# First two passes of an expert loop taken out ahead of the loop, with shared-expert work behind the first pass's gate and up products

## What is computed

```python
def swiglu(t, wg, wu, wd):
    return (jax.nn.silu(t @ wg) * (t @ wu)) @ wd
...
    def expert_block(args):
        tok, wb, e = args
        xb = t_pad[tok]
        yb = swiglu(xb, w_e_gate[e], w_e_up[e], w_e_down[e])
        return yb * wb[:, None]
...
    routed = jax.ops.segment_sum(yb.reshape(P, d), slot_tok, num_segments=T + 1)[:T]
    shared = swiglu(t, w_sh_gate, w_sh_up, w_sh_down)
    return (routed + shared).astype(h.dtype).reshape(b, n, d)
```

## Time and profile before

| what | value |
|---|---|
| median of 3 runs (lowest, highest) | 1037.86 us (1037.82 to 1041.65) |
| the profiled execution | 1042.4 us, its span 1040.6 us |
| busy in the span: PE, DVE, ACT, POOL | 944.7, 513.2, 330.9, 400.1 us |
| chain that ended last | PE 46%, DMA 43%, DVE 4%, SP's queue 4% |
| HBM read, written | 282.15 MB, 39.32 MB |

### The profile page before, as it was taken

How to read it: one execution, slowest core, us unless ns; L and a number is a source line. 1 busy time by engine, 2 the same in 40 slices (tenths; PEclk the granted TensorE clock), 3 DMA queues, 4 the chain that set the end, 5 groups by cost and what they waited for, 6 DMA issues and landing times.

```text
span 1040.6 us, 13867 instructions
## 1 busy us (share of the span) xinstructions
PE 944.7 (91%) x3980; PEld 388.6 (37%) x3981; DVE 513.2 (49%) x682; ACT 330.9 (32%) x595; POOL 400.1 (38%) x300
## 2 busy tenths in 40 slices
PE   3999999899999989979999898996999999999760
PEld 0554444466555553323333232332333333333220
DVE  2336876777156954434545344442445455454234
ACT  4212222377345422222232232322222323322232
POOL 0312431000000045553556644554455565555531
PEclk9999999999999999989999999998999999999895
DMA  9955452900314967999989999999999999999837
GB/s 368 350 181 202 167 198 71 363 1 2 122 81 156 356 230 284 394 388 377 382 294 339 397 381 370 373 357 367 387 377 362 352 354 372 370 355 366 308 71 243
DMA packets 63180, 298.29 MB, mean 287 GB/s; under 512 B 15189, under 2 KB 15905, under 8 KB 35121
## 3 DMA queue, kind: packets, MB, share of 16 engines
q1 hardware_dynamic: 42130, 258.01, 63.2%
q0 software_dynamic: 19024, 35.68, 14.2%
q10 hardware_dynamic: 2000, 4.28, 1.1%
HBM read 282.15 MB, written 39.32 MB: 309 GB/s over the span
## 4 chain that ended last, share of the span: by engine, by line
PE 46%; DMA 43%; DVE 4%; SPq 4%; issue 3%; ACT 1%; POOL 0%; ACTq 0%; POOLq 0%; DVEq 0%
DMA wring<-in_w_e_down 33%; PE psum L944 13%; PE psum L1186 10%; DMA wring<-in_w_e_up 5%; PE psum L1198 5%; PE psum L1034 3%; PE psum L981 3%; PE psum L1014 3%; PE psum L1005 2%; DMA ring<-in_w_ada 2%; SPq L451 2%; PE psum L1148 2%; DMA expert_sums<-xres,sidx 2%; SPq L427 1%; PE psum L899 1%
## 5 line engine op out<-in xcount | busy, mean ns | idle before, releaser
L1186 PE MATMUL psum<-wring,xres 128*64 x832 | 379.9, 611 | 35.5 <-DVE cur_g L1613 34.2
L1186 PE MATMUL psum<-cur_g,xres 128*64 128x512 f32 x832 | 379.9, 611 | 0.0
L554 POOL DMA_INDIRECT xg<-h_rows,gidx x216 | 249.6, 1156 | 219.4 <-ACT gidx L801 141.0
L1186 PEld LDWEIGHTS psum<-wring,xres 128*64 128x64 f32 x832 | 112.5, 140 | 258.4 <-issue 253.0
L1198 PE MATMUL psum<-wring,rows 128*64 x424 | 190.6, 592 | 1.9 <-ACT rows L797 1.9
L1198 PE MATMUL psum<-rows 128*64 128x512 f32 x424 | 190.7, 592 | 0.0
L1617 DVE STREAM_TRANSPOSE xres<-xg 128x1024 f32<-128x1024 f32 x53 | 108.5, 2047 | 160.9 <-DMA xg<-h_rows,gidx 158.7
L1613 DVE COPY cur_g<-wring 128x1536 f32 x106 | 125.7, 1228 | 46.3 <-SPq L440 46.3
L561 POOL DMA_INDIRECT expert_sums<-xres,sidx x54 | 95.4, 1767 | 96.9 <-DMA expert_sums<-xres,sidx 85.7
L862 ACT COPY xres<-psum 128x1024 f32<-128x1024 f32 x53 | 53.6, 1012 | 190.4 <-PE psum L1198 103.1
L1186 PEld LDWEIGHTS psum<-cur_g,xres 128*64 128x64 f32 x832 | 112.5, 140 | 0.0
(11 more groups left out here) (241 smaller groups left out, 870.1 us busy)
## 6 DMA issues: line engine op xcount, KB each, us to landing
wring<-in_w_e_gate SPq DMA_DIRECT2D x64, 1024.0 KB, 8.4
wring<-in_w_e_up SPq DMA_DIRECT2D x64, 1024.0 KB, 16.1
wring<-in_w_e_down SPq DMA_DIRECT2D x64, 1024.0 KB, 18.2
ring<-in_w_ada SPq DMA_DIRECT2D x20, 1024.0 KB, 5.1
ring<-in_w_in SPq DMA_DIRECT2D x4, 2048.0 KB, 29.1
heads<-in_w_ada SPq DMA_DIRECT2D x4, 1024.0 KB, 23.3
ring<-in_w_out SPq DMA_DIRECT2D x1, 4096.0 KB, 15.2
xg<-h_rows,gidx POOLq DMA_INDIRECT x216
```

Source lines behind the costliest of these rows:

```text
L554: pool.indirect_dma_start(xg[q][:, 256 * s:256 * s + 256], None, hrows, bass.IndirectOffsetOnAxis(gidx[:, q, s:s + 1].bitcast(U32), 0), bo ...
L1186: last = pe.matmul(pp[2][SUB * g:SUB * g + SUB, 512 * q:512 * q + 2 * F] .rearrange("p (u f) -> p u f", u=2), xT[:, q, k, SUB * g:SUB * g ...
```

## The change

PE: passes 0 and 1 are written out ahead of the loop, which now begins at pair 2. Pass 0 is gate and up alone; the absent pair's turn and down product are gone. `shared_hidden(3)` and `shared_down(3)` stand behind gate and up of pair 0 instead of ahead of it. ACT follows the same order: row numbers of gather 2 and the SiLU of pair 0 first, then `shared_keep(3)` and `shared_rows(3)`, then the wait for the stores, then the copies of pair 0's down weights. SP: load 6 also waits until gather 0 has landed (`s_gt[0]` at 64). DVE: the product of pair p's hidden values also waits for the turn of those before (`s_ht`). The last shared turn and down product count 2 instead of 1, so that all later counts stay as they were. POOL is unchanged, its wait for all four shared stores included.

```diff
@@ -491,6 +491,7 @@
                     down_arrived(n - 3)
                 if n == NB:
                     sp.wait_ge(s_gu, NT)
+                    sp.wait_ge(s_gt[0], 64)
                 else:
                     if n == NB + 1:
                         sp.wait_ge(s_tab, 1)
@@ -845,31 +846,44 @@
             shared_keep(2)
             shared_silu(3)
             shared_rows(1)
-            shared_keep(3)
             shared_rows(2)
-            shared_rows(3)
             act.wait_ge(s_idx, 1)
             act.wait_ge(s_tab, 1)
-            act.sem_inc(s_cdn, FJ)
             nb = act.value_load(ntab[0:1, 0:1], min_val=E, max_val=MAXB - 1)
             pairs = act.snap((nb + 1) // 2)
-            for n in range(1, NT):
-                act.wait_ge(s_sh_st[n], 16)
 
             def keep_y(n, q, scattered):
                 act.wait_ge(s_dn, n)
                 act.wait_ge(s_scat, scattered)
                 act.copy(ysb[:, q], pp[q]).then_inc(s_yev, 1)
 
-            with act.Fori(0, pairs, 2) as i:
+            def open_pass(p, q):
+                gather_index(p + 2, q)
+                w = down_weights(p)
+                act.wait_ge(s_gu, p + (NT + 1))
+                act.activation(sg, pp[2][:, 512 * q:512 * q + F], ACT.Silu).then_inc(s_sil, 1)
+                return w
+
+            def close_pass(p, q, w):
+                keep_y(p + (NT + 1), 1 - q, p * 16 + 16)
+                scatter_index(p - 1, 1 - q)
+                copy_down(*w)
+
+            w = open_pass(0, 0)
+            shared_keep(3)
+            shared_rows(3)
+            act.sem_inc(s_cdn, FJ)
+            for n in range(1, NT):
+                act.wait_ge(s_sh_st[n], 16)
+            act.sem_inc(s_yev, 1)
+            scatter_index(-1, 1)
+            copy_down(*w)
+            w = open_pass(1, 1)
+            close_pass(1, 1, w)
+            with act.Fori(2, pairs, 2) as i:
                 for q in range(2):
-                    gather_index(i + (q + 2), q)
-                    e, w0 = down_weights(i + q)
-                    act.wait_ge(s_gu, i + (q + NT + 1))
-                    act.activation(sg, pp[2][:, 512 * q:512 * q + F], ACT.Silu).then_inc(s_sil, 1)
-                    keep_y(i + (q + NT + 1), 1 - q, i * 16 + (16 * q + 16))
-                    scatter_index(i + (q - 1), 1 - q)
-                    copy_down(e, w0)
+                    w = open_pass(i + q, q)
+                    close_pass(i + q, q, w)
             turns = act.snap((pairs + 1) // 2)
             n_down = act.snap(turns * 2 + (NT + 1))
             n_scattered = act.snap(turns * 32 + 16)
@@ -1155,7 +1169,7 @@
                     pe.wait_ge(s_hte, n)
                 for j in range(FJ):
                     last = pe.transpose(pp[1][:, 512 + j * P:512 + (j + 1) * P], hmid_sh[:, j:F:FJ], ident)
-                last.then_inc(s_ht, 1)
+                last.then_inc(s_ht, 2 if n == NT - 1 else 1)
 
             def shared_down(n):
                 pe.wait_ge(s_hte, n + 1)
@@ -1170,7 +1184,7 @@
                     for j in range(FJ):
                         last = pe.matmul(o[:, 512 * m:512 * m + 512], hT_sh[:, n % 2, j, :],
                                          w[:, j, 512 * m:512 * m + 512], start=(j == 0), stop=(j == FJ - 1))
-                last.then_inc(s_dn, 1)
+                last.then_inc(s_dn, 2 if n == NT - 1 else 1)
 
             def weights_of(p):
                 e = pe.value_load(tab[0:1, bass.ds(p * 2 + 2, 1)], min_val=0, max_val=E - 1)
@@ -1232,24 +1246,37 @@
             shared_gate_up(3, range(5, KD))
             shared_down(1)
             shared_down(2)
-            shared_hidden(3)
-            shared_down(3)
             pe.wait_ge(s_tab, 1)
             nb = pe.value_load(ntab[0:1, 0:1], min_val=E, max_val=MAXB - 1)
             pairs = pe.snap((nb + 1) // 2)
+
+            def open_pass(p, q, w):
+                pe.wait_ge(s_xte, p + 1)
+                pe.wait_ge(s_w, w[0] + 2)
+                gate_up(p, q, w[1])
+
+            def full_pass(p, q, before, w):
+                pe.wait_ge(s_hm, p + NT)
+                turn_hidden(1 - q)
+                open_pass(p, q, w)
+                pe.wait_ge(s_hte, p + NT)
+                pe.wait_ge(s_yev, p + (NT - 1))
+                down(p * 2 + 1, 1 - q, *before)
+
+            w0 = weights_of(0)
+            pe.wait_ge(s_hm, NT)
+            open_pass(0, 0, w0)
+            shared_hidden(3)
+            shared_down(3)
+            w1 = weights_of(1)
             pe.wait_ge(s_yev, NT - 1)
-            with pe.Fori(0, pairs, 2) as i:
-                for q in range(2):
-                    before = (e, w0) if q else weights_of(i - 1)
-                    e, w0 = weights_of(i + q)
-                    pe.wait_ge(s_hm, i + (q + NT))
-                    turn_hidden(1 - q)
-                    pe.wait_ge(s_xte, i + (q + 1))
-                    pe.wait_ge(s_w, e + 2)
-                    gate_up(i + q, q, w0)
-                    pe.wait_ge(s_hte, i + (q + NT))
-                    pe.wait_ge(s_yev, i + (q + NT - 1))
-                    down(i * 2 + (2 * q + 1), 1 - q, *before)
+            full_pass(1, 1, w0, w1)
+            with pe.Fori(2, pairs, 2) as i:
+                before = weights_of(i - 1)
+                w = weights_of(i)
+                full_pass(i, 0, before, w)
+                w1 = weights_of(i + 1)
+                full_pass(i + 1, 1, w, w1)
             turns = pe.snap((pairs + 1) // 2)
             n_down = pe.snap(turns * 2 + NT)
             pe.wait_ge(s_hm, n_down)
@@ -1628,6 +1655,7 @@
                     e, w0 = gate_up_weights(i + (q + 1))
                     turn_block(1 - q, i * 32 + 64 * (q + 1))
                     dve.wait_ge(s_sil, i + (q + NT + 1))
+                    dve.wait_ge(s_ht, i + (q + NT))
                     dve.scalar_tensor_tensor(hmid, sg, slot_w[:, bass.ds(i + q, 1)],
                                              pp[2][:, 512 * q + F:512 * q + 2 * F], ALU.mult, ALU.mult)\
                        .then_inc(s_hm, 1)
```

## The result

| | before | changed |
|---|---|---|
| median of 16 runs each (lowest, highest) | 1039.12 us (1034.73 to 1043.42) | 1049.06 us (1044.11 to 1052.85) |
| the profiled execution, its span | 1042.4, 1040.6 us | 1047.97, 1045.9 us |

The ratio is 1.0097, 95% interval 1.0081 to 1.0112: 1% **slower**, 9.9 us. The forecast was 1036.5 in a range to 1041. The stage of the passes also begins 1.65 us earlier in the changed trace (first piece of gather 0 at 373.12, before 374.77); where it matters I count from that start, "from the stage's start".

What follows compares the result with a forecast made beforehand. Weight loads were taken to pace the passes, with PE full beside them. Of 4.1 us gained at the head, the late store and its waiters left 1.4 at pass 7: 1036.5 us, range 1031 to 1041.

Steps and rivals of the forecast that it cites:

- Gather 0 without g6: Head of the passes: with load 6 held back, the first gather lands at 382.7 us instead of 386.73.
- the 4.1: Head of the passes: gate and up of pair 0 start 4.1 us earlier, at 385.2.
- The upper bound of 5.2 us: Pass 0's start: most it could gain, if the gather lands at once and PE starts 1.1 us earlier.
- The store's landing: Shared tile 3's store among the weights: 4.9 us in flight, landing at 402.8, 11.7 us later than before.
- those two: The two earlier shared stores under load, one with load 6's weights under way, whose median of 4.9 us was taken.
- The other end of the bounds, 9.0: Slow end for tile 3's store: 9.0 us, as a store took with loads 4 and 5 under way.
- Who stands behind it: Behind tile 3's store: ACT's down-weight copies and POOL's gather 2, so pass 2 begins 7.2 us later, at 418.2.
- The forecast's 1.4 us gained: Start of pass 7: 474.6 us against 476.02 before.
- The rival of the slow store: Tile 3's store ends with the weights, 9.0 us; pass 7 2.7 us later than before, 1040.6 us; chance 0.2.
- The weights behind d9: Before pass 6: 9 load parts from load 9's down weights to load 13's gate and up take 30.7 us.
- Everything behind pass 7 therefore moves with pass 7's start, us for us: From pass 7 to the kernel's end: any shift of pass 7's start reaches the end in full.

Runs made afterwards that it cites:

- e3: Changed kernel with gather 2 ahead of POOL's wait for the stores and tile 3 in another buffer, freeing ACT's down-weight copies: 1043.76 us, 1.0041.
- e10: Changed kernel with the store of shared tile 3 issued from SP's queue instead of ACT's, between two weight loads: 1049.08 us, 1.007.
- e2: Changed kernel with gather 2 issued ahead of POOL's wait for the shared stores: 1047.62 us, 1.0073.
- e9: Changed kernel with SP holding load 8's gate and up weights back until tile 3's store has landed: 1049.95 us, 1.0087.
- e12: Changed kernel with tile 3's store in SP's queue and gather 2 ahead of POOL's wait: 1046.39 us, 1.006.
- e13: e3 with empty scatters reading a free buffer and POOL waiting for tile 3's store only at its loop: 1040.53 us, 1.0007.
- e1: Changed kernel with the last shared turn and down product, copy and store back ahead of pass 0: 1038.55 us, 0.9992.
- e5: Changed kernel without SP's new wait of load 6 for gather 0: 1052.93 us, 1.0122.
- e7: Kernel before the change, with only SP's new wait of load 6 for gather 0 added: 1040.99 us, 1.0014.
- e4: Kernel before the change, with POOL entering its loop only when gate and up of pair 1 have ended: 1048.63 us, 1.0092.

## Why the prediction was wrong

- **Gather 0 without g6.** Forecast: the last piece's issue shrinks from 1.85 to 0.99 us and it lands 2.5 behind. POOL took 1.85 us for that piece again, and it landed 4.79 us after the piece's start, not 3.46: 2.7 us gained of the 4.1. The starting times (382.4 against my 382.7) agree only because this execution's stage began 1.65 us earlier; that is luck. The upper bound of 5.2 us was also too low by its own rows: had the gather landed at once, PE would have been free at 383.06, 6.1 us earlier.
- **Clock at pass 0 (not foreseen).** I gave pass 0's gate and up 7.0 us. With the shared down product gone from ahead of it, PE was idle for 3.54 us, and the products then took 8.78 with a granted clock of 0.66 in the stretch (the level of 1.2 GHz for part of it). That took 1.8 of what was left; the store was issued at 399.41, not 397.9. The low clock is no fixed price of the order: seven traces have PE idle for 3.48 to 3.54 us ahead of pass 0, and gate and up took 8.48 to 9.80 us in three of them (the changed kernel, e3, e10) and 7.1 in four (e2, e9, e12, e13). In the whole head, 370 to 430 us, the clock stood at its lower level for 10.2 us in the changed trace and for none before (1 less the granted clock, doubled, over windows of 1 us), each time behind an idle stretch of PE. So part of what the waits cost is paid as slow products.
- **The store's landing: the step that failed first.** "I take 4.9, for the queue is then about as full as at those two": it took 8.49. The other end of the bounds, 9.0, was the right row. Wherever tile 3's store went under load, it took 7.0 to 9.4 us (e1, e2, e3, e5, e7, e9, e10, e12). The 4.9 was the median of 5.7 and 4.0, so "no store under load was below 4.9" misread it; during the second of them the DMA share fell from 0.92 (384 to 386 us) to 0.37 (388 to 390), so that store flew on emptying engines.
- **Who stands behind it.** Both queues were named, and both waited: POOL 23.6 us, ACT 8.7. The third, the empty scatter and ACT's buffer behind it, was not named. Down of pair 0 was forecast directly behind pass 1's gate and up, at 404.3; it came at 409.67, at low clock. d7 went at 415.06 and not 407.8, and from 410 to 415 nothing was loaded.
- **Pass 7, the wrong sign.** The forecast's 1.4 us gained rest on the 4.9 us. From the stage's start the store landed 6.75 us later than forecast: 3.6 by its flight, 1.8 by the clock, 1.4 by gather 0. From the landing to pass 2 it was then 11.9 us and not 15.4, since gather 2 met empty DMA engines and landed in 2.11 us; this error ran the other way and hid a part of the first. From pass 2 to pass 7 it was 1.7 us more than forecast. Pass 7 came 3.5 us later than before. The rival of the slow store gave +2.7 and nearly had it.
- **The weights behind d9.** Forecast 30.7 us from d9's issue to g13 in place. DVE's copy of g13, which had waited for it, began at 465.84, 33.8 us behind d9 (432.04), and pass 6 at 467.00, 35.0 behind. In e4 and e7 pass 6 began 34.2 us behind d9. My estimate from these: with the forecast's own d9 (430.7) pass 6 would begin at 464.9 to 465.7 and not at 463.7, so little or nothing is left of the 1.4 us, even with the store at 4.9.
- **"Everything behind pass 7 therefore moves with pass 7's start, us for us": the step that put the result outside the range.** With the rival's 9.0 us for the store the sum gave 1040.6, inside 1031 to 1041; pass 7 came 3.5 us late and the kernel 9.9. From pass 7 to pass 51 it was 514.9 us before and 518.0 in the changed trace; 517.3 in e9, 517.4 in e4, 517.7 in e5, but 514.4 in e1 and 512.6 in e13. It isn't a matter of a late POOL alone: e2 has 514.7 and a loss, e7 517.8 and an unchanged median. Nor does pass 7's start tell the end: from the stage's start it came 101.2 us behind before and in e3, and e3 is 0.4% slower; in e1 and e7 it came 3.1 us earlier and nothing was gained. These are single traces, but they agree that the shift at pass 7 was not the shift at the end.

The loop's waits (line, waited for, us in total, times, longest; 450 to 1000 us), before and then changed:

```profile
DVE xres L1617 <- DMA xg<-h_rows,gidx: 141.1, 36, 6.7
...
ACT xres L862 <- DMA expert_sums<-xres,sidx: 87.3, 20, 6.8
```

```profile
DVE xres L1644 <- DMA xg<-h_rows,gidx: 188.9, 39, 7.6
...
ACT xres L858 <- DMA expert_sums<-xres,sidx: 160.7, 31, 7.7
```

DVE waits longer for gathers and ACT for scatters, and PE is busy for 489.9 us between 480 and 1000, against 494.3 before. But these waits don't follow the loss: e1, which is as fast as before, has 165.0 and 133.5 us of them, and e2, which is 0.7% slower, has 134.3 and 62.1, less than before. So they can't be called its cause. Why the loop adds to the head's loss is **open**: no experiment here touches the loop.

The head's loss can be seen in another count: the time in which the DMA engines were short of full (1 less the share, over windows of 1 us, 370 to 445 us) was 16.7 us before, 21.7 with the change, 22.4 in e4 and 27.0 in e5, but 12.9 in e1 and 13.2 in e13. These slow kernels starve the engines in the head by 5 us or more beyond before. But e3, 0.4% slower, has 17.4, hardly more than before, and e1 and e13 starve them by 3.5 to 3.8 less and gain nothing that can be measured, so this count isn't the time either. Also open: the 2.9 us that e9's store took beyond the bytes ahead of it.

## What to carry to other kernels

Moving a transfer from idle DMA engines into a full weight stream changes its landing time, here threefold: price it with the slowest row under load, not the median, and look at what is issued ahead of it. Then list every instruction of every queue behind its semaphore, the ones that the diff doesn't touch first, empty work and the buffers it holds among them, and ask of each whether its data needs that transfer at all. And where the products of an absent item are dropped, look at which latency they covered: here 1.2 us of 3.9 came out.

## What the runs showed of the hardware

- Tile 3's store of 512 KB took 2.6 us on idle DMA engines (before) and 7.0 to 9.4 us behind loads of 1024 KB, alike from ACT's queue (8.49, changed kernel) and from SP's (7.05, e10), and hardly less where the next load was held back (7.89, e9). Tile 2's took 3.9 us when issued 0.37 us ahead of a load (changed kernel) and 9.5 when issued 0.21 us behind it (e1).
- A scatter with no row in bounds took 8.79 us to land under load (e3), and ACT's copy into its source buffer waited for that landing.
- POOL's fourth piece of the first gather took 1.85 us with g6 under way (before) and without (changed kernel); its neighbours took 1.0 to 1.4.
- Behind 3.48 to 3.54 us of an idle PE, pass 0's gate and up took 8.48 to 9.80 us in three traces (the lower clock for part of the time) and 7.1 us at full clock in four: the same idle time cost the clock in some executions and not in others.
